# Loading x from ScalarE's own queue, and the last half of a weight chunk as two loads

## What is computed

```python
c_act = jax.nn.silu(c)
mod = c_act @ w_ada[l] + b_ada[l]
shift1, scale1, gate1, shift2, scale2, gate2 = jnp.split(mod, 6, axis=-1)

h = modulate(x, norm_mix_g[l], shift1, scale1)
proj = h @ w_in[l]
u_pool = proj[..., :POOL_WIDTH]
qkv = proj[..., POOL_WIDTH:POOL_WIDTH + 3 * ATTN_WIDTH]
gates = proj[..., POOL_WIDTH + 3 * ATTN_WIDTH:]
...
x = x + gate1[:, None, :] * (merged @ w_out[l])

h2 = modulate(x, norm_ffn_g[l], shift2, scale2)
x = x + gate2[:, None, :] * peer_ffn(h2, peer_wq[l], peer_sub_keys[l], peer_u[l], peer_v[l])
```

## Time and profile before

| | us |
|---|---|
| median of 3 runs | 1170.68 |
| lowest and highest run | 1170.68, 1174.07 |
| span of the profiled execution | 1172.4 |
| TensorE matmul busy in it | 1041.2 (89%) |
| VectorE busy | 826.7 (71%) |
| ScalarE busy | 423.2 (36%) |
| GpSimd busy | 290.3 (25%) |

### The profile page before, as it was taken

How to read it: one execution, slowest core, us unless ns; L and a number is a source line. 1 busy time by engine, 2 the same in 40 slices (tenths; PEclk the granted TensorE clock), 3 DMA queues, 4 the chain that set the end, 5 groups by cost and what they waited for, 6 DMA issues and landing times.

```text
span 1172.4 us, 13740 instructions
## 1 busy us (share of the span) xinstructions
PE 1041.2 (89%) x5066; PEld 702.4 (60%) x5066; DVE 826.7 (71%) x1912; ACT 423.2 (36%) x895; POOL 290.3 (25%) x262
## 2 busy tenths in 40 slices
PE   5999999898999996886886878788899999999997
PEld 3799976644555543432332323333389878999986
DVE  5699765768767768778887555555566878888843
ACT  3545622322332222222222111111266665665631
POOL 0000001444354543353544444445000000000000
PEclk8999999999999998898988999989999999999999
DMA  9977594999999999899999999999994443554530
GB/s 367 427 319 297 239 399 158 418 401 422 420 419 420 421 422 421 365 410 421 422 421 421 422 421 422 420 422 422 384 396 180 145 179 134 198 209 163 197 144 37
DMA packets 48199, 390.46 MB, mean 333 GB/s; under 512 B 5498, under 2 KB 5890, under 8 KB 7300
## 3 DMA queue, kind: packets, MB, share of 16 engines
q0 software_dynamic: 37040, 269.51, 55.5%
q1 hardware_dynamic: 11092, 120.07, 26.1%
HBM read 388.50 MB, written 1.06 MB: 332 GB/s over the span
## 4 chain that ended last, share of the span: by engine, by line
PE 52%; DMA 31%; DVE 11%; ACT 3%; issue 2%; POOL 1%; SPq 1%; DVEq 0%
DMA ring<-in_uv,idx 27%; PE ps L1457 18%; PE ps L1801 15%; PE ps L1958 5%; DMA ring<-in_w_ada 4%; DVE ring L1243 3%; PE ps L1669 2%; PE ps L1611 2%; PE ps L1886 2%; PE ps L1481 1%; PE ps L1684 1%; DVE ring_r L885 1%; POOL ring L514 1%; PE ps L1510 1%; DVE ring L896 1%
## 5 line engine op out<-in xcount | busy, mean ns | idle before, releaser
L1801 PE MATMUL ps<-ring,probT 128*128 128x512 f32 x1020 | 490.7, 625 | 103.6 <-ACT probT L759 102.1
L1243 DVE CUSTOM_DVE_ANT_0 ring<-h2t,ring 128x1024 f32<-128x1024 f32 x255 | 308.7, 1222 | 166.0 <-DMA ring<-in_uv,idx 165.8
L1801 PEld LDWEIGHTS ps<-ring,probT 128*128 128x128 f32 x1020 | 192.6, 199 | 338.8 <-issue 194.7
L514 POOL DMA_INDIRECT ring<-in_uv,idx x255 | 287.9, 1129 | 339.1 <-PE ps L1801 287.0
L1457 PE MATMUL ps<-util_r,ring_r 128*128 128x256 f32 x1312 | 216.9, 282 | 0.0
L1457 PEld LDWEIGHTS ps<-util_r,ring_r 128*128 128x128 f32 x1312 | 181.6, 189 | 1.3 <-issue 1.1
L885 DVE TENSOR_TENSOR ring_r<-ring,ring_r 128x1024 fp32r<-128x1024 f32 x134 | 157.7, 1220 | 34.0 <-ACT ring_r L536 33.9
L754 ACT ACTIVATE prob<-prob 128x2 f32<-128x2 f32 (+2 forms) x98 | 20.0, 204 | 368.5 <-DVE prob L1243 368.4
L536 ACT ACTIVATE ring_r<-ring 128x1024 fp32r<-128x1024 f32 x134 | 133.6, 1050 | 41.5 <-DMA ring<-in_w_in 19.3
L1457 PE MATMUL ps<-h_r,ring_r 128*128 128x256 f32 x704 | 126.1, 282 | 0.1
L759 ACT ACTIVATE probT<-ct,prob 128x128 f32<-128x128 f32 x256 | 85.5, 392 | 76.5 <-DVE prob L1249 75.8
(11 more groups left out here) (213 smaller groups left out, 980.4 us busy)
## 6 DMA issues: line engine op xcount, KB each, us to landing
ring<-in_w_in SPq DMA_DIRECT2D x12, 2048.0 KB, 13.8
ring<-in_w_up SPq DMA_DIRECT2D x11, 2048.0 KB, 7.9
ring<-in_w_ada SPq DMA_DIRECT2D x7, 2048.0 KB, 9.8
ring<-in_w_down SPq DMA_DIRECT2D x6, 2048.0 KB, 7.7
ring<-in_w_ada SPq DMA_DIRECT2D x8, 1024.0 KB, 16.4
ring<-in_w_out SPq DMA_DIRECT2D x4, 2048.0 KB, 8.0
ring<-in_w_q SPq DMA_DIRECT2D x3, 2048.0 KB, 11.3
ring<-in_w_br SPq DMA_DIRECT2D x2, 2048.0 KB, 13.1
```

Of the source, the lines that this page charges most:

```text
L514: e.indirect_dma_start(out=row_buf[n], out_offset=None, in_=uv, in_offset=bass.IndirectOffsetOnAxis(ap=idx[:, tt, k:k + 1], axis=0)).then_inc(
L1243: e.tensor_tensor_reduce(u, h2t[:, tt, :], u, 1.0, 0.0, ALU.mult, ALU.add, av[:, tt, n % 128:n % 128 + 1]).then_inc(*made.put(("dot", n)))
L1801: ins = e.matmul(acc[half][:, :], diag[:, n % 8, :], row_buf[n][:, D + half * 512:D + (half + 1) * 512], start=(k == 0), stop=(k == 127))
```

## The change

SP no longer issues the load of x; ScalarE does, as the first instruction of its program. The second half of chunk 3 of `w_ada` comes as two loads of 1024 numbers per partition, the first with a new semaphore `ada3`, the last with the chunk's own; VectorE's third product of chunk 3 waits for `ada3` and its fourth for the chunk's.

```diff
-        once = {n: Mark(sem("s_" + n), 16) for n in ("ct", "ct2", "cl", "x", "c", "bands", "wp", "wf", "rb", "bk", "gf", "g1", "b1", "g2", "b2")}
+        once = {n: Mark(sem("s_" + n), 16) for n in ("ada3", "ct", "ct2", "cl", "x", "c", "bands", "wp", "wf", "rb", "bk", "gf", "g1", "b1", "g2", "b2")}
...
             e.dma_start(cl[:, :], cols).then_inc(*once["cl"].put(0))
-            e.dma_start(x_sb[:, :, :].rearrange("p k t -> p (k t)"), x_in).then_inc(*once["x"].put(0))
             def load_half(kind, i, z):
...
             load_half("in", 0, 0)
-            for kind, i in (("ada", 1), ("ada", 3)):
-                load_half(kind, i, 0)
-                load_half(kind, i, 1)
+            load_half("ada", 1, 0)
+            load_half("ada", 1, 1)
+            load_half("ada", 3, 0)
+            third, last = slice(2 * D, 3 * D), slice(3 * D, 4 * D)
+            e.dma_start(slots[3][:, third], w_ada[3][:, third]).then_inc(*once["ada3"].put(0))
+            e.dma_start(slots[3][:, last], w_ada[3][:, last]).then_inc(*loaded[3].put(("ada", 3)))
             load_half("in", 0, 1)
...
+            e.dma_start(x_sb[:, :, :].rearrange("p k t -> p (k t)"), x_in).then_inc(*once["x"].put(0))
             for half in range(2):
                 act.wait_ge(done, ("c row", 1))
...
                 for j in js:
-                    dve.wait_ge(half_loaded["ada", c] if c < 4 and j < 2 else loaded[SLOT_OF["ada", c]], ("ada", c))
+                    if (c, j) == (3, 2):
+                        dve.wait_ge(once["ada3"], 0)
+                    else:
+                        dve.wait_ge(half_loaded["ada", c] if c < 4 and j < 2 else loaded[SLOT_OF["ada", c]], ("ada", c))
```

## The result

The change made the kernel slower by a little: a median of 1174.43 us in 20 runs (1172.46 to 1177.95) against 1172.24 in 20 runs of before (1170.54 to 1176.04). The ratio is 1.0015, with a 95% interval of 1.0008 to 1.0022, so 0.9 to 2.6 us. The forecast was 1170.4, a gain of 0.3, and its range ended at 1174.1. The runs also spread over many values between these, so the grain of 3.39 us that the first three seemed to have does not exist.

What follows compares the result with a forecast made beforehand. Row gathers and TensorE bound the kernel; the opening's gain, decided at 85.2 us, carries to the end. min(0.7, 0.28) = 0.3 us off 1170.68 gave 1170.4 us, range 1167.3 to 1174.1.

Steps and rivals of the forecast that it cites:

- grain of 3.39 us: Run times: three runs hinted at a clock step of 3.3933 us; the range added one step either side of the median.
- V: VectorE's chain from chunk 4's landing at 56.33 to the operand releasing TensorE at 85.21; said to end last, gaining s.
- T: TensorE's chain, busy from 40 to 84.9 us, going back to the first projection's second half; 0.22 us of slack.
- The expression for T: T, through VectorE's sixteen products of chunks 0 to 3: gains 1.76 - d while that is less than 1.1 + s.
- d: Opening: delay of ct's landing from sharing the DMA engines with x; taken as 1.7 us, bounds 0.3 and 2.9.
- The whole sum: Gain at 85.2 us, the smaller of V's and T's: min(s, 0.22 + 1.76 - d) = 0.3 us.
- rival B: Ct's landing: constants starve and the kernel is slower, 1171.2 or 1171.6 us, from d = 1.98 on; chance 0.15.
- its first way: Rival B at ct's landing: ct waits for the whole of x, d = 2.46, a loss of 0.5 us, 1171.2.
- The slack of 0.22: At 85.21 us: TensorE's idle time before VectorE's operand releases it, so T could lose 0.22 us unseen.
- s: Opening: how much earlier the DMA stream starts with x requested sooner; taken as 0.7 us, from nothing to 1.28.
- 33.55 - 1.1 - s: Split load of chunk 3: latest time at which transfers bind T, third product starting one product (1.14 us) sooner.
- slower by over 0.3%: Whole kernel: more than 3.5 us slower, needing the worst case and a clock step together; chance 0.04.

Runs made afterwards that it cites:

- before, third: The kernel before, no edit, profiled a third time for its opening; scores at 84.57 us, no separate timed result given.
- x behind ct: Changed kernel, but ScalarE waits for ct to land before issuing x; 1174.78 us, ratio 1.0026.
- four pieces: Changed kernel, but ScalarE issues x as four loads of 256 KB, cut by columns; 1173.26 us, ratio 1.0007.
- ct and x: Changed kernel, but ct's load moves from SP to ScalarE, ahead of x; 1171.64 us, ratio 1.0001.
- ct and x, again: Changed kernel with ScalarE issuing ct and then x, run once more for its time; 1171.73 us, ratio 0.9989.
- split alone: Changed kernel with x back on SP, only the last half of chunk 3 split in two loads; 1172.78 us, ratio 1.0000.

## Why the prediction was wrong

**What held.** The place where the change is decided, and the two chains. Two distances give TensorE's scores. V is chunk 4's first product plus 28.86 us (85.21 - 56.35, from before). T is the column matmul plus 43.55 (85.80 - 42.26, from the changed kernel, with 0.01 for rounding); the column matmul is the first one of the projections in three passes, right behind the first projection. The scores start at the later of the two:

| kernel | column matmul | chunk 4 | T | V | scores |
|---|---|---|---|---|---|
| before | 41.38 | 56.35 | 84.93 | 85.21 | 85.21 |
| before, third | 40.66 | 55.71 | 84.21 | 84.57 | 84.57 |
| changed | 42.26 | 54.50 | 85.81 | 83.36 | 85.80 |
| x behind ct | 42.98 | 54.95 | 86.53 | 83.81 | 86.53 |
| four pieces | 41.32 | 54.98 | 84.87 | 83.84 | 84.86 |
| ct and x | 39.67 | 54.53 | 83.22 | 83.39 | 83.39 |
| ct and x, again | 39.52 | 54.01 | 83.07 | 82.87 | 82.86 |
| split alone | 41.23 | 55.61 | 84.78 | 84.47 | 84.60 |

The last two rows miss by 0.2 us, in T: its starting point is good to no more than that. The other five profiles agree within 0.02.

The expression for T held too: 1.76 - 2.64 = -0.88, and the column matmul moved from 41.38 to 42.26, 0.88 later. But 0.1 us of that agreement is luck. VectorE's eighth product moved by 0.79 only; the rest seems to come from TensorE, which ran without a pause from the first half of the projection into the second, where it had stood idle for 2.16 us before. The prediction had let that first half move by d; its last weight load moved from 31.66 to 34.94, by 3.28, since more of it fell into the stretch at half clock. The whole sum with the measured terms is min(1.85, 0.22 - 0.88) = -0.66; the two traces show -0.59.

**The step that failed: d, the delay of the constants.** "I take 1.7, by the row in which two queues compete." It was 2.64, and all of it was the wait for ct's first row, which moved at 4.84 instead of 2.10 us; turns had no part in it. The row was rightly read, but it shows two queues whose rows are both at the engines already, one of them GpSimd's. It says nothing of the time between a request and its first row, and there the runs show SP's and ScalarE's requests in one line. This put the case over the 1.98 us that rival B named, and by its first way: the loss of 0.5 for ct behind the whole of x against 0.6 in the two traces. The prediction had priced that way and given all of B a chance of 0.15; the 2.64 lies within its own bounds for d, 0.3 to 2.9. The Trainium skill, page "DMA: Bandwidth & Descriptors", section "Queues, rings and completion order", has an engine drain a packet of many descriptors before it switches; in the changed kernel it comes out as that rule says, but the run with x behind ct speaks against it as the cause: there x's 128 rows, eight to an engine, were spread over 5.4 us among about as many of the other queue.

**The reference.** The slack of 0.22 and the point 85.21 came from one execution, and I took them as fixed. Repeated, the same program reached the scores 0.6 and 1.1 us sooner, because both chains then hung on the start of the stream. The changed kernel does not profit from that, since ct holds it up. So the loss at the scores was 1.2 us by the means, and not 0.6.

**s was too low, and did not matter.** Taken as 0.7, at most 1.28; chunk 4 came 1.85 sooner than in the first trace and 0.8 and 1.2 sooner than in the other two. The rule of the same page, section "Issuing engines are not separate DMA queues", would have had 0.47. The traces do not agree: the engines carried 403 GB/s from 3.2 to 4.4 us instead of 139, so more was gained than the time of issuing.

**The split.** Worth nothing, as forecast, but the term "33.55 - 1.1 - s" left out the half chunk before it; 0.3 was to be had.

**Chances and range.** The share of "slower by over 0.3%" was right to be small, since 1.0015 is half of that. The range missed by 0.3 us at the top because it was built on the median of three runs, 1170.68; twenty runs of the same kernel gave 1172.24. I explained the spread by a grain instead of allowing for it; without that added step the range would have ended at 1172.1.

## What to carry to other kernels

Before a large load goes to a second queue "for free", look at what small load the opening waits for, and keep the small one's request ahead of the large one's, on whichever queue: ct landed in 2.2 us again that way. A load that was not late is not worth moving for its own sake; here the gain lay in the start of the stream, and the opening kept it once ct went first, 1.5 us at the scores, while the time did not show it clearly. A slack of 0.2 us in one trace is not a number to build on: take two or three profiles where a term is smaller than their spread.

## What was not expected of the hardware

- Two hardware queues do not start independently. A request of 137.5 KB made 0.4 us after one of 1 MB on the other queue moved no row while 0.99 MB of the other passed (4.9 us to landing instead of 2.2). A request of 1 MB on an empty queue moved none for 3.7 us behind requests of the other.
- The start of the first transfers varies from one execution to the next: 261, 309 and 296 GB/s from 3.2 to 6.7 us for one program, and its scores 0.6 and 1.1 us apart from the slowest.
